# Layer 1 of a two-layer decoder: two low-rank inputs computed ahead of the norm, and the sample states of two heads read by one product

## The chip, the core and the metric

The kernel runs on one core of one Trainium2 chip. A core has TensorE (PE: matrix products, with its weight loads shown apart as PEld), VectorE (DVE), ScalarE (ACT), GpSimd (POOL) and SyncE (SP, which here issues most of the transfers). Engines run side by side and wait for one another on semaphores. TensorE writes to PSUM, which has 8 banks; the kernel numbers its PSUM results ("groups") through the program and gives group g the bank g mod 8. The metric is the device time of one execution in microseconds (us).

## What is computed

A two-layer trunk over 288 tokens of width 1024: 256 of one prompt and 32 of 8 samples with 4 tokens each. Layer 0 is a state-space and attention mixer with a dense feed-forward block; layer 1 is an RWKV-7 mixer with a mixture of 8 experts. The change lies in the layer 1 mixer, of which this is the part that matters:

```python
prev = jnp.concatenate([shift0[:, None].astype(h.dtype), h[:, :-1]], axis=1)   # h = rms(x) * norm_mix[1]
xx = prev - h
xr, xw, xk, xv, xa, xg = [h + xx * mu[i] for i in range(6)]
r = xr @ wr
k = xk @ wk
v = xv @ wv
w_log = -jax.nn.softplus(-(w0 + jnp.tanh(xw @ w1) @ w2).astype(f32)) - 0.5
a = jax.nn.sigmoid((a0 + (xa @ a1) @ a2).astype(f32))
g = jax.nn.sigmoid(xg @ g1) @ g2
...
def step(S, inp):                       # per sample and head, S is 64 x 64
    sa = jnp.einsum('bhvk,bhk->bhv', S, a_t)
    S = S * w_t[:, :, None, :] + sa[..., None] * b_t[:, :, None, :] + v_t[..., None] * k_t[:, :, None, :]
    return S, jnp.einsum('bhvk,bhk->bhv', S, r_t)
```

w1 and a1 are 1024 x 64, g1 is 1024 x 128; all is in 32-bit floats. Each mixed input is a share (1 - mu) of the token's own h and a share mu of the h of the token before it (of the stored shift state for the first token of a sample, of nothing for the first of the prompt).

## The kernel before

Activations lie feature-major: 8 tiles of 128 features by 288 tokens (KT = 8, T = 288, TP = 256 prompt tokens). Each engine runs a fixed list in its own order, so what stands first in the list goes first, and later entries wait behind it. PSUM groups are numbered by `stage` in one list (lines 515 to 530), and a group can be written when the group eight numbers before it has been freed. In the code `full(eng, g)` waits until TensorE has filled group g, `emptied(eng, g)` until a reader has freed it.

**The start of layer 1.** The last down projection of layer 0 (groups FD10, m = 0 to 7) is added to x tile by tile on DVE (`residual`, L1559). ACT squares each tile (L1017), DVE sums the squares (L1503), TensorE sums over the partitions in one product with ones (group N3), ACT makes the inverse root rs (L1028 Ln, L1031 Exp), and DVE writes h = x * norm * rs (L1493), the eight signals `h_tile`. DVE then copies the tokens that are shifted (L1849 to L1855). For the six mixed inputs n = 0 to 5 (w, a, g, k, r, v) ACT writes the own share into one of two buffers, `xi[n % 2]` (`own_share`, L1234), and DVE adds the share of the token before (`mix`, L1863 for the prompt, L1864 for the samples), signal `xi_ready`. TensorE takes them as they come: Hw (xw by w1), Ha (xa by a1), Rw (8 groups, the tanh of Hw by w2), Hg, Ra (8), Rg (8), then eight columns Rk0 to Rk7 of xk by wk, 16 records each, then r and v. ACT reads the hidden groups (L1240) and the outputs (L1247 with a sigmoid for w and a, L1249 for g). Its order is: own share 0, 1; hidden w; own share 2; hidden a; outputs w; own share 3; hidden g; outputs a; own share 4; outputs g.

Matrix products of 32-bit floats appear as two records each on PE and PEld, so 8 products give 16 records.

**The sample states.** Near the end of the mixer, the group sZY reads the 16 heads x 8 samples of states against the 4 tokens of a sample, for two vectors (2 x 4 = 8 columns). Two heads share 128 partitions, `r0` = 0 or 64:

```python
for i in range(KT):
    for s in range(DB):
        for r0 in (0, 64):
            ins = mm(zy[r0:r0 + 64, i * DB + s], wk[r0:r0 + 64, i, s, :],
                     AR[r0:r0 + 64, i, :, TP + DL * s:TP + DL * (s + 1)])
```

ACT copies the group out in two instructions (L1354, L1355). Ahead of it DVE masks the groups sA and sX (L1998, L2004), makes a constant and scales two inputs (`sE`, L2028, L2030) and adds a prompt state (L1984, L1991); behind it TensorE goes on with QZ(3,1), three transposes (L2650) and the rest of the chain. Then come the output projection and the experts, which fill the span from about 957 us on.

## Time and profile before

| | |
|---|---|
| median of 3 runs | 1747.38 us (1741.54 to 1748.83) |
| profiled execution | 1750.27 us, span of its core 1748.6 us |
| TensorE busy | 1683.8 us, 96% of the span |
| mean granted TensorE clock | 0.967 of full |
| chain of waits | PE 89%, DVE 7%, ACT 2% |

The page gives busy time by engine, the granted clock and the chain that ended last. Since one engine fills 96% of the span, what matters is where it waits, where its clock is halved, and what it is given to do. A timeline shows instructions in order of time, merged when alike: start, length from the first start to the last end, engine, line, operation, what is written from what, shape and count; in brackets the idle time before it and who ended it. For TensorE the shape 64\*128 means weights of 64 rows (partitions) by 128 columns.

### The profile page before, as it was taken

To read this page: it belongs to the slowest core of one execution; us is meant where nothing else is said; L and a number is where in the kernel's file an instruction comes from. 1 tells how busy PE (TensorE), PEld (TensorE's weight loads), DVE (VectorE), ACT (ScalarE), POOL (GpSimd) and SP (SyncE) were. 2 spreads that over 40 slices of the span, in tenths; PEclk is the share of its full clock that TensorE was granted. 3 is DMA by queue.
4 is the path that set the end of the run, shared out by engine and by line. 5 is a ranking of instruction groups with operands and counts; after the bars stand their busy time and mean duration, and the time that the engine had idled before them with its cause. 6 is when DMAs were issued, how large, how long until landed. Compare 5 with 4: busy or idle time off the path is not lost.

```text
span 1748.6 us, 25799 instructions
## 1 busy us (share of the span) xinstructions
PE 1683.8 (96%) x10101; PEld 1393.0 (80%) x10101; DVE 1177.0 (67%) x1525; ACT 918.6 (53%) x1193; POOL 148.0 (8%) x180
## 2 busy tenths in 40 slices
PE   9999699999997899999999999999999999999999
PEld 7776477999995677999867787888878787878787
DVE  5652722677657454444444788979797989888897
ACT  3442521543327243433223577767686868777774
POOL 1102100000000013322021200000000000000011
PEclk9999879999998999999797899999999999999999
DMA  8832422554322330000024989989797989899893
GB/s 349 356 133 86 199 97 103 224 194 155 145 86 97 123 118 0 2 1 2 2 103 169 393 335 380 411 326 423 313 427 312 423 355 383 356 380 392 348 421 142
DMA packets 41097, 405.03 MB, mean 232 GB/s; under 512 B 4784, under 2 KB 5072, under 8 KB 11664
## 3 DMA queue, kind: packets, MB, share of 16 engines
q1 hardware_dynamic: 34336, 372.64, 53.0%
q0 software_dynamic: 6672, 31.14, 4.4%
q8 instruction: 64, 1.05, 0.2%
q14 instruction: 25, 0.20, 0.0%
HBM read 379.49 MB, written 26.30 MB: 232 GB/s over the span
## 4 chain that ended last, share of the span: by engine, by line
PE 89%; DVE 7%; ACT 2%; issue 1%; DMA 1%; DVEq 0%; ACTq 0%; SPq 0%; POOL 0%; POOLq 0%
PE ps L2260 85%; DVE rest_ring L2072 1%; DMA ring<-in_moe_w 1%; PE ps L3010 1%; PE ps L2702 1%; PE ps L2650 1%; DVE ring L1553 0%; DVE arena L1522 0%; DVE arena L1648 0%; ACT arena L1151 0%; PE ps L2963 0%; DVE arena L1531 0%; PE ps L2928 0%; DVE arena L1661 0%; DVE arena L1527 0%
## 5 line engine op out<-in xcount | busy, mean ns | idle before, releaser
L2260 PE MATMUL ps<-head,hsel 128*128 128x512 f32 x1408 | 458.9, 397 | 4.5 <-DVE rest_ring L2072 4.5
L2072 DVE TENSOR_TENSOR rest_ring<-ring,head 128x2048 fp32r<-128x2048 f32 (+1 forms) x160 | 328.0, 2070 | 6.6 <-ACT head L1384 6.5
L2260 PEld LDWEIGHTS ps<-head,hsel 128*128 128x128 f32 x1408 | 265.0, 188 | 63.9 <-DVE rest_ring L2072 7.8
L2260 PE MATMUL ps<-arena,ring 128*128 128x288 f32 (+9 forms) x1552 | 276.8, 350 | 10.1 <-DVE arena L1864 6.6
L1384 ACT ACTIVATE head<-ring 128x2048 fp32r<-128x2048 f32 (+1 forms) x160 | 274.3, 1741 | 18.9 <-DMA ring<-in_moe_w 18.7
L2260 PEld LDWEIGHTS ps<-arena,ring 128*128 128x128 f32 (+4 forms) x1552 | 214.1, 200 | 69.8 <-issue 17.1
L2260 PE MATMUL ps<-rest_ring,hsel 128*128 128x512 f32 x576 | 225.0, 391 | 0.0
L2260 PE MATMUL ps<-head,actT_split 128*128 128x512 f32 x512 | 168.8, 393 | 7.4 <-issue 5.6
L2260 PE MATMUL ps<-rest_arena,head 128*128 128x288 f32 x704 | 174.7, 296 | 0.0
L2260 PE MATMUL ps<-rest_arena,rest_ring 128*128 128x288 f32 x528 | 155.5, 294 | 0.0
L2260 PE MATMUL ps<-h,ring 128*128 128x288 f32 (+2 forms) x624 | 135.2, 374 | 1.8 <-DVE h L1493 1.8
L2260 PEld LDWEIGHTS ps<-h,ring 128*128 128x128 f32 (+2 forms) x624 | 100.9, 179 | 35.7 <-issue 8.6
L2260 PEld LDWEIGHTS ps<-rest_ring,hsel 128*128 128x128 f32 x576 | 108.7, 189 | 20.8
L2260 PEld LDWEIGHTS ps<-rest_arena,head 128*128 128x128 f32 x704 | 122.5, 188 | 0.1
L2260 PEld LDWEIGHTS ps<-head,actT_split 128*128 128x128 f32 x512 | 96.1, 188 | 31.3 <-issue 8.4
L1559 DVE TENSOR_TENSOR x<-x,ps 128x288 f32<-128x288 f32 x110 | 48.7, 453 | 107.1 <-PE ps L2260 106.9
L2066 DVE TENSOR_TENSOR rest_ring<-ring,head 128x2048 fp32r<-128x2048 f32 x48 | 109.7, 2285 | 9.7 <-ACT head L1379 9.6
L2260 PE MATMUL ps<-arena 64*64 64x64 f32 (+12 forms) x1178 | 104.5, 295 | 10.7 <-DVE arena L1681 3.1
L2260 PE MATMUL ps<-rest_ring,actT_split 128*128 128x512 f32 x288 | 112.2, 390 | 0.0
L2260 PE MATMUL ps<-hsel,head 128*128 128x288 f32 x352 | 103.8, 295 | 0.0
L2260 PEld LDWEIGHTS ps<-arena 64*64 64x64 f32 (+6 forms) x1178 | 75.8, 164 | 30.3 <-issue 23.6
L2260 PEld LDWEIGHTS ps<-rest_arena,rest_ring 128*128 128x128 f32 x528 | 99.5, 188 | 0.0
(364 smaller groups left out, 2402.4 us busy)
## 6 DMA issues: line engine op xcount, KB each, us to landing
ring<-in_moe_w SPq DMA_DIRECT2D x72, 2048.0 KB, 11.1
ring<-in_moe_w SPq DMA_DIRECT2D x72, 1024.0 KB, 7.5
arena<-in_moe_w SPq DMA_DIRECT2D x16, 2048.0 KB, 14.3
ring<-in_ffn_w SPq DMA_DIRECT2D x11, 2048.0 KB, 7.4
arena<-in_moe_w SPq DMA_DIRECT2D x16, 1024.0 KB
ring<-in_ffn_w SPq DMA_DIRECT2D x11, 1024.0 KB, 5.0
moe_rows<-arena POOLq DMA_DIRECT2D x1, 6656.0 KB, 33.8
ring<-in_w_in SPq DMA_DIRECT2D x2, 3072.0 KB, 13.1
```

The lines of the kernel that those rows point to most:

```text
L1384: A(mhead[c % 2][:, o:o + w], mslot[s][:, o:o + w], ACT.Copy).then_inc(sem("gu_head"), 1)
L1559: V.tensor_tensor(x[:, m, :], x[:, m, :], bank(g)[:, 0:T], ALU.add).then_inc(freesem(g), 1)
L2066: V.tensor_tensor(mrest[s][:, GU:SLOT], mslot[s][:, GU:SLOT], down_head(c).bitcast(F32), ALU.subtract).then_inc(sem("dn_split"), 1)
L2072: V.tensor_tensor(mrest[s][:, o:o + w], mslot[s][:, o:o + w], mhead[c % 2][:, o:o + w].bitcast(F32), ALU.subtract).then_inc(sem("gu_split" ...
L2260: return nc.tensor.matmul(o, l, r, start=start, stop=stop, skip_group_check=skip)
L2650: ins = nc.tensor.transpose(b[0:rows, i * P:(i + 1) * P], src[:, 4 * hf + i, t0:t0 + rows], ident)
L2702: ins = nc.tensor.transpose(b[:, n * P:(n + 1) * P], (Mi if lv else Mti)[gg % 2][:, 4 * q + n, :], ident)
L3010: ins = nc.tensor.transpose(turned(c)[:, u * P:(u + 1) * P], actm[c % 2][:, u * P:(u + 1) * P], ident)
```

## The change

**Hidden products ahead of the norm.** rs is one number per token, so it can be multiplied in after the product. For w and a, ACT writes raw = x * norm into `xi[0]` beside each square. DVE makes from w1 and from a1 one 128-column weight each: 64 columns scaled by 1 - mu, 64 by mu (four instructions, placed in the last pass but one over the feed-forward chunks). One product of 288 columns per tile gives both shares of all tokens, one of 8 columns the shift state's share. DVE (`joined_hidden`) scales both halves by rs and adds the second, shifted by one token, to the first. Own shares and mixes of w and a are gone. The tanh moves to its own instruction on ACT; Ra stands before Hg.

**sZY.** DVE clears and fills `ar_both`, in which each head's 8 columns stand beside 8 columns of zeros, so one product with weights of 128 rows by 64 columns gives both heads of a pair of partitions (16 columns). ACT copies out in eight instructions.

```diff
@@ scalar
-            squares(sq3, x, lambda k: emptied(act, base[f"FD{FC - 1}"] + k), "sq_ready")
+            for k in range(KT):
+                emptied(act, base[f"FD{FC - 1}"] + k)
+                A(sq3[:, k, :], x[:, k, :], ACT.Square).then_inc(sem("sq_ready"), 1)
+                A(raw[:, k, :], x[:, k, :], ACT.Copy, scale=v("nm1", k)).then_inc(sem("h_head"), 1)
...
-            own_share(0)
-            own_share(1)
-            hidden("w", ACT.Tanh)
+            emptied(act, base["Hw"])
+            A(hid[0][0:64, :], hid[0][0:64, :], ACT.Tanh).then_inc(sem("hid_tanh"), 1)
             own_share(2)
-            hidden("a", ACT.Copy)
             lora_out("w", sw, "w0")
+            lora_out("a", aT, "a0")
             own_share(3)
             emptied(act, base["Rw"] + 7)
             hidden("g", ACT.Sigmoid)
-            lora_out("a", aT, "a0")
             own_share(4)
             lora_out("g", gT, None)
...
+                    zy = bank(g).rearrange("p (i b r a l) -> p i b r a l", b=DB, r=2, a=2, l=DL)
+                    for i_, dst in enumerate((z1T, y1)):
+                        for u in range(2):
+                            for r in range(2):
+                                ins = A(dst[64 * r:64 * r + 64, u:KT:2, :].rearrange("p k (b l) -> p k b l", l=DL),
+                                        zy[64 * u:64 * u + 64, :, :, r, i_, :], ACT.Copy)
@@ vector
+                if c == FC - 1:
+                    loaded(dve, "lora")
+                    o = VEC["mu"][0]
+                    for nm, mrow, at in (("w", 1, 0), ("a", 4, 512)):
+                        for i, share in enumerate((ommu[:, 8 * mrow:8 * mrow + 8], vec[:, o + 8 * mrow:o + 8 * mrow + 8])):
+                            V.tensor_tensor(both_shares(nm)[:, :, i, :], W("lora")[:, at:at + 512].rearrange("p (k n) -> p k n", k=KT),
+                                            share.unsqueeze(2).broadcast_to([P, KT, 64]), ALU.mult).then_inc(sem("shares_ready"), 1)
...
+            def joined_hidden(nm, dst):
+
+                g = base["H" + nm]
+                full(dve, g)
+                b = bank(g)
+                old = prev_hid[:, TP:T].rearrange("p (b l) -> p b l", l=DL)
+                V.tensor_tensor(prev_hid[:, 1:TP], b[64:P, 0:TP - 1], rs[0][64:P, 0:TP - 1], ALU.mult)
+                V.tensor_tensor(old[:, :, 1:DL], b[64:P, TP:T].rearrange("p (b l) -> p b l", l=DL)[:, :, 0:DL - 1],
+                                rs[0][64:P, TP:T].rearrange("p (b l) -> p b l", l=DL)[:, :, 0:DL - 1], ALU.mult)
+                V.tensor_copy(old[:, :, 0], b[64:P, T:T + DB])
+                link(V.tensor_tensor(dst[0:64, :], b[0:64, 0:T], rs[0][0:64, :], ALU.mult))
+                V.tensor_tensor(dst[0:64, 1:T], dst[0:64, 1:T], prev_hid[:, 1:T], ALU.add).then_inc(freesem(g), 1)
+                emptied(dve, g)
...
+            joined_hidden("w", hid[0])
+            for k in range(KT):
+                V.scalar_tensor_tensor(h[:, k, :], x[:, k, :], v("nm1", k), rs[0], ALU.mult, ALU.mult).then_inc(sem("h_tile"), 1)
+            joined_hidden("a", hid[1])
...
-            for n in range(5):
-                mix(n)
+            mix(2)
+            V.tensor_copy(shiftout[:, :, 0], h[:, :, TP - 1]).then_inc(sem("shiftout_ready"), 1)
+            V.tensor_copy(shiftout[:, :, 1:9], hs[:, :, :, 3]).then_inc(sem("shiftout_ready"), 1)
+            mix(3)
+            mix(4)
...
+                    for r in range(2):
+                        V.memset(ar_both[64 * r:64 * r + 64, :, 1 - r], 0.0)
+                        V.tensor_copy(ar_both[64 * r:64 * r + 64, :, r], AR[64 * r:64 * r + 64, :, :, TP:T]).then_inc(sem("ends_scaled"), 1)
@@ tensor
+            pe.wait_ge(sem("shares_ready"), 4)
+            pe.wait_ge(sem("x_half_loaded"), 32)
+            both_hidden("w")
+            summed(base["N3"], 2, sq3, C("ones"))
+            both_hidden("a")
             lora_out(0, "w")
+            lora_out(1, "a")
+            loaded(pe, "lora")
             hidden(2, "g")
-            lora_out(1, "a")
             lora_out(2, "g")
...
+                    pe.wait_ge(sem("ends_scaled"), 2)
+                    zy = b.rearrange("p (n r a l) -> p n r a l", r=2, a=2, l=DL)
                     for i in range(KT):
                         for s in range(DB):
-                            for r0 in (0, 64):
-                                ins = mm(zy[r0:r0 + 64, i * DB + s], wk[r0:r0 + 64, i, s, :],
-                                         AR[r0:r0 + 64, i, :, TP + DL * s:TP + DL * (s + 1)])
+                            r0 = 64 * (i % 2)
+                            ins = mm(zy[r0:r0 + 64, i // 2 * DB + s], wk[:, i, s, :], ar_both[:, i, :, :, DL * s:DL * (s + 1)])
```

The order of TensorE around the norm of layer 1, before; the last rows of the feed-forward block, N3 (one product with the constants `cst`), then Hw and Ha (64x288) and Rw, Hg, Ra, Rg and the first columns' products (128x288):

```order
L2260 MATMUL ps<-rest_arena,head 128x288 x2
L2260 MATMUL ps<-rest_arena,rest_ring 128x288
L2260 MATMUL ps<-arena,cst 128x288
L2260 MATMUL ps<-arena,ring 64x288 x16
L2260 MATMUL ps<-arena,ring 128x288 x48
```

And of the change, the same place; the pair of rows with `shiftst` stands eight times ahead of N3 and eight times behind it:

```order
L2306 MATMUL ps<-rest_arena,head 128x288 x2
L2306 MATMUL ps<-rest_arena,rest_ring 128x288
L2306 MATMUL ps<-arena,ring 128x288
L2306 MATMUL ps<-shiftst,ring 128x8
...
L2306 MATMUL ps<-arena,cst 128x288
L2306 MATMUL ps<-arena 128x288
L2306 MATMUL ps<-shiftst,arena 128x8
...
L2306 MATMUL ps<-arena,ring 128x288 x48
```

Hw now stands ahead of N3 and Ha behind it, both with 128 weight columns, and neither waits for h any longer.

The order of ACT from the inverse root (`rs`) to the outputs of g, before:

```order
L1031 ACTIVATE rs<-rs 128x288
L1035 ACT_TABLE_LOAD
L1234 ACTIVATE arena<-h,arena 128x288 x16
L1240 ACTIVATE arena<-ps 64x288
L1234 ACTIVATE arena<-h,arena 128x288 x8
L1240 ACTIVATE arena<-ps 64x288
L1247 ACTIVATE arena<-ps,vec 128x288 x8
L1234 ACTIVATE arena<-h,arena 128x288 x8
L1240 ACTIVATE arena<-ps 128x288
L1247 ACTIVATE arena<-ps,vec 128x288 x8
L1234 ACTIVATE arena<-h,arena 128x288 x8
L1249 ACTIVATE arena<-ps 128x288 x8
```

And of the change:

```order
L1041 ACTIVATE rs<-rs 128x288
L1045 ACT_TABLE_LOAD
L1264 ACTIVATE arena<-arena 64x288
L1246 ACTIVATE arena<-h,arena 128x288 x8
L1259 ACTIVATE arena<-ps,vec 128x288 x16
L1246 ACTIVATE arena<-h,arena 128x288 x8
L1252 ACTIVATE arena<-ps 128x288
L1246 ACTIVATE arena<-h,arena 128x288 x8
L1261 ACTIVATE arena<-ps 128x288 x8
```

Sixteen own-share rows are gone, and the hidden row of g (L1252) now stands behind both sets of sigmoids and an own share.

## Rows read from the trace of the kernel before

**Rows 1.** The page: busy time, share of the span and instructions by engine.
```profile
PE 1683.8 (96%) x10101; PEld 1393.0 (80%) x10101; DVE 1177.0 (67%) x1525; ACT 918.6 (53%) x1193; POOL 148.0 (8%) x180
```
**Rows 2.** Stretches: length, then busy PE, PEld, DVE, ACT, POOL, clock, DMA.
```profile
533.60:539.70 6.10, 0.00 (x0) 0.00 (x0) 5.37 (x22) 6.04 (x13) 0.55 (x1) 0.50 0.69 293
539.70:543.80 4.10, 4.03 (x9) 2.07 (x10) 4.10 (x15) 2.69 (x7) 0.00 (x0) 0.50 0.01 2
543.80:549.50 5.70, 5.70 (x25) 3.08 (x23) 5.70 (x22) 3.63 (x9) 0.00 (x0) 1.00 0.00 0
```
**Rows 3.** Timeline of PE around the norm: start, length, instruction, idle before.
```profile
530.13 0.29 PE L2260 MATMUL ps<-rest_arena,rest_ring 128*128 128x288 f32 x1
532.40 0.75 PE L2260 MATMUL ps<-arena,cst 128*128 128x288 f32 x2 [1.98 <-DVE arena L1503]
539.77 26.25 PE L2260 MATMUL ps<-arena,ring 128*64 128x288 f32 x96 [6.62 <-DVE arena L1864]
566.26 4.12 PE L2260 MATMUL ps<-arena,ring 128*128 128x288 f32 x16 [0.25 <-issue]
```
**Rows 4.** Timeline of DVE, last splits, residuals, norm, and copies.
```profile
518.39 0.88 DVE L1835 TENSOR_TENSOR rest_arena<-arena,rest_arena 128x288 fp32r<-128x288 f32 x2
519.19 0.81 DVE L1559 TENSOR_TENSOR x<-x,ps 128x288 f32<-128x288 f32 x2
...
524.18 0.45 DVE L1559 TENSOR_TENSOR x<-x,ps 128x288 f32<-128x288 f32 x1 [0.34 <-PE ps L2260]
...
534.26 3.52 DVE L1493 SCALAR_TENSOR_TENSOR h<-x,vec,rs 128x288 f32<-128x288 f32 x8 [1.92 <-ACT rs L1031]
```
**Rows 5.** Timeline of ACT, own shares, outputs with sigmoid, hidden g.
```profile
550.42 3.90 ACT L1247 ACTIVATE arena<-ps,vec 128x288 f32<-128x288 f32 x8 [0.28 <-PE ps L2260]
554.22 3.50 ACT L1234 ACTIVATE arena<-h,arena 128x288 f32<-128x288 f32 x8
557.96 0.41 ACT L1240 ACTIVATE arena<-ps 128x288 f32<-128x288 f32 x1 [0.23 <-PE ps L2260]
```
**Rows 6.** Timeline of PEld, the loads of Rw and Hg.
```profile
549.64 3.69 PEld L2260 LDWEIGHTS ps<-arena,ring 64*128 64x128 f32 x16 [0.44 <-issue]
553.71 3.69 PEld L2260 LDWEIGHTS ps<-arena,ring 128*128 128x128 f32 x16 [0.39 <-issue]
```
**Rows 7.** Timeline of PEld, weight loads with few columns to multiply: four places.
```profile
842.78 0.58 PEld L2260 LDWEIGHTS ps<-arena 64*32 64x32 f32 x32
...
846.30 12.69 PEld L2260 LDWEIGHTS ps<-arena,ring 64*64 64x64 f32 x255
...
875.95 1.08 PEld L2260 LDWEIGHTS ps<-ring 32*32 32x32 f32 x32
...
929.32 3.20 PEld L2260 LDWEIGHTS ps<-router,h 128*128 128x128 f32 x28 [0.81 <-issue]
```
**Rows 8.** Stretches around sZY, columns as in Rows 2.
```profile
846.30:847.60 1.30, 1.30 (x53) 1.30 (x51) 0.98 (x3) 0.00 (x0) 0.00 (x0) 1.00 0.00 0
847.60:859.00 11.40, 11.40 (x217) 11.38 (x214) 3.86 (x7) 0.00 (x0) 0.00 (x0) 0.50 0.01 3
859.00:868.00 9.00, 9.00 (x47) 6.30 (x47) 4.93 (x9) 4.78 (x9) 0.00 (x0) 0.50 0.00 0
```
**Rows 9.** Timeline of DVE and ACT around sZY.
```profile
844.40 0.29 DVE L2028 SCALAR_TENSOR_TENSOR arena<-cst 128x128 f32<-128x128 f32 x1
...
846.57 0.85 DVE L1984 TENSOR_TENSOR h<-ring,ps 64x256 f32<-64x256 f32 x2 [1.21 <-PE ps L2260]
...
848.34 0.68 DVE L2036 TENSOR_TENSOR ring<-arena,cst 32x512 f32<-32x512 f32 x1
...
859.13 0.38 ACT L1354 ACTIVATE arena<-ps 128x256 f32<-128x256 f32 x1 [13.11 <-PE ps L2260]
...
862.91 0.59 ACT L1298 ACTIVATE h<-ps 64x512 f32<-64x512 f32 x1 [3.12 <-PE ps L2260]
```

More of the change, by code:

```diff
@@ L277, in decoder_trunk @@
         hid = tm1
+        raw = xi[0]
+        prev_hid = Us[0:64, 0:T]
         xxf = xx[:, :, :].rearrange("p k t -> p (k t)")
@@ L287, in decoder_trunk @@
         centre = xxf[:, 2048:2048 + P]
+        ar_both = AR[:, :, 1, 0:P].rearrange("p k (r a t) -> p k r a t", r=2, a=2)
         def gn_unit(n):
@@ L366, in decoder_trunk, with both_shares @@
         slots = ar[:, 3 * SLOT + 3 * P:3 * SLOT + 4 * P]
+        def both_shares(nm):
+            o = (where["lora"] % RING) * SLOT + 5120
+            t = ring[:, o:o + 1024] if nm == "w" else xi2[:, KT * T:KT * T + 1024]
+            return t.rearrange("p (k s n) -> p k s n", k=KT, s=2)
         def down_head(c):
@@ L517, in decoder_trunk @@
         stage("N3", 1)
-        for name, n in (("Hw", 1), ("Ha", 1), ("Rw", 8), ("Hg", 1), ("Ra", 8), ("Rg", 8)):
+        for name, n in (("Hw", 1), ("Ha", 1), ("Rw", 8), ("Ra", 8), ("Hg", 1), ("Rg", 8)):
             stage(name, n)
@@ L1352, in _ @@
                     full(act, g)
-                    zy = bank(g).rearrange("p (n a l) -> p n a l", a=2, l=DL)
-                    A(z1T.rearrange("p k (b l) -> p (k b) l", l=DL), zy[:, :, 0, :], ACT.Copy)
-                    A(y1.rearrange("p k (b l) -> p (k b) l", l=DL), zy[:, :, 1, :], ACT.Copy).then_inc(freesem(g), 1)
+                    zy = bank(g).rearrange("p (i b r a l) -> p i b r a l", b=DB, r=2, a=2, l=DL)
[4 more added lines that the diff above has]
+                                        zy[64 * u:64 * u + 64, :, :, r, i_, :], ACT.Copy)
+                    ins.then_inc(freesem(g), 1)
                 elif name == "sVT":
@@ L1844, in _ @@
             sum_squares(sq3, 24, KT - 1)
-            norm(base["N3"], "nm1", "h_tile")
+            def joined_hidden(nm, dst):
[10 more added lines that the diff above has]
+                emptied(dve, g)
+            emptied(dve, base["N3"])
+            n_norm[0] += 1
+            dve.wait_ge(sem("rs_ready"), n_norm[0])
+            joined_hidden("w", hid[0])
+            for k in range(KT):
+                V.scalar_tensor_tensor(h[:, k, :], x[:, k, :], v("nm1", k), rs[0], ALU.mult, ALU.mult).then_inc(sem("h_tile"), 1)
+            joined_hidden("a", hid[1])
             dve.wait_ge(sem("h_tile"), 2 * KT)
             dve.wait_ge(sem("x_half_loaded"), 32)
-            V.tensor_copy(shiftout[:, :, 0], h[:, :, TP - 1]).then_inc(sem("shiftout_ready"), 1)
             hs = h[:, :, TP:T].rearrange("p k (b l) -> p k b l", l=DL)
-            V.tensor_copy(shiftout[:, :, 1:9], hs[:, :, :, 3]).then_inc(sem("shiftout_ready"), 1)
             hp = hprev.rearrange("p k (b l) -> p k b l", l=DL)
@@ L1891, in _ @@
             mix(5)
-            dve.wait_ge(sem("xi_ready"), 48)
+            dve.wait_ge(sem("xi_ready"), 32)
             for t in range(KT):
@@ L2598, in _ @@
                         done(ins, g)
-            summed(base["N3"], 2, sq3, C("ones"))
-            loaded(pe, "lora")
             lw = W("lora")
@@ L2604, in _, with both_hidden @@
             l2 = {"w": 2048, "a": 3072, "g": 4096}
+            shift_now = shiftst
+            def both_hidden(nm):
+                g = base["H" + nm]
+                w = both_shares(nm).rearrange("p k s n -> p k (s n)")
+                b = take(g)
+                for k in range(KT):
+                    if nm == "w":
+                        pe.wait_ge(sem("h_head"), KT + k + 1)
+                    mm(b[:, 0:T], w[:, k, :], raw[:, k, :], k == 0, k == KT - 1, skip=True)
+                    ins = mm(b[:, T:T + DB], w[:, k, :], shift_now[:, k, :], False, k == KT - 1, skip=True)
+                done(ins, g)
             def hidden(n, nm):
@@ L2607, in hidden @@
                 w = lw[:, o:o + KT * rows].rearrange("p (k n) -> p k n", k=KT)
-                proj(base["H" + nm], w, 0, rows, xi[n % 2], rows=rows, ready="xi_ready", n0=8 * n)
+                proj(base["H" + nm], w, 0, rows, xi[n % 2], rows=rows, ready="xi_ready", n0=8 * (n - 2))
             def lora_out(n, nm):
@@ L2612, in lora_out @@
                 emptied(pe, base["H" + nm])
+                if nm == "w":
+                    pe.wait_ge(sem("hid_tanh"), 1)
                 for m in range(KT):
@@ L2616, in lora_out @@
                     done(mm(b[:, 0:T], lw[0:rows, l2[nm] + m * P:l2[nm] + (m + 1) * P], hid[n % 2][0:rows, :]), g)
-            hidden(0, "w")
-            hidden(1, "a")
+            pe.wait_ge(sem("shares_ready"), 4)
[3 more added lines that the diff above has]
+            both_hidden("a")
             lora_out(0, "w")
+            lora_out(1, "a")
+            loaded(pe, "lora")
             hidden(2, "g")
-            lora_out(1, "a")
             lora_out(2, "g")
@@ L2633, in column @@
                 w = W(f"w{nm}{t // 4}").rearrange("p (k n) -> p k n", k=KT)
-                proj(g, w, t % 4 * P, P, xi[n % 2], ready=None if t else "xi_ready", n0=8 * n)
+                proj(g, w, t % 4 * P, P, xi[n % 2], ready=None if t else "xi_ready", n0=8 * (n - 2))
             for t in range(KT):
```

15 lines of the change are left out of this document (7 added, 8 removed).

## The prediction

> **What bounds the kernel.** I read the page first: TensorE is busy in 96% of the span [rows 1]. A change can pay only where that engine waits, where it runs at half clock, or where it gets less to do. The timeline of PE shows one such place at the start of layer 1: between the last product of layer 0 (530.13 + 0.29 = 530.42) and the first column Rk0 (566.26) lie 35.84 us, in which it waits 1.98 us for the sum of squares and 6.62 us for norm, own share and mix [rows 3]. The stretches say more: the clock falls to 0.50 (1.2 instead of 2.4 GHz) in the gap and is still there in the first 4.1 us of Hw and Ha [rows 2]. From 543.8 on TensorE is full. The second place is sZY: 255 records fill 12.69 us [rows 7], nearly all at clock 0.50, and 9.0 us behind it are at 0.50 too [rows 8]. From 566 to 840 nothing is touched, so what is won at Rk0 is passed on as a shift.
>
> **Part one, step by step.** The steps are dated from 530.42, at full clock.
> Hw: each tile is two records of 288 columns and two of 8. The first cost 4.12 / 16 = 0.26 [rows 3], rather 0.25 with the pipeline's tail off. The second are nowhere beside long ones; the nearest row has 128 weight columns against 8 columns and takes 3.20 / 28 = 0.114 each [rows 7]. Bounds are 0 (the load hides behind the long product) and 0.114; I take the upper, since behind a short product the next load has no cover. 8 x (0.50 + 0.23) = 5.8 us, to 536.2. This is work where there was a gap. Its raw tiles come in time: square and scaled copy take less than the 0.8 us that the next residual needs.
> N3 now stands behind Hw and starts at 536.2 instead of 532.40: the norm is put off by 3.8 us. From the start of N3 to the start of the norm it was 534.26 - 532.40 = 1.86 us [rows 3, 4], so rs is there at 538.1. DVE joins w in five instructions, two of them full rows and one of 255 columns (near 0.45, as a residual [rows 4]), two tiny: 1.6 us, bounds 1.2 and 2.5; then tanh, 0.4. All of this is under Ha, which runs from 536.7 to 542.5.
> From there ACT sets the pace. Its list is own share 2 (it overwrites the raw tiles, so it waits for Ha), 16 sigmoids, own share 3, hidden g: 3.5 + 2 x 3.8 + 3.5 + 0.4 = 15.0 us (3.8 is the step from 550.42 to 554.22) [rows 5], from 542.6 to 557.6. TensorE meanwhile does Rw, then Ra as ACT frees banks (to 550.5), then Hg, 4.1 us (553.71 - 549.64 [rows 6]), to 554.6. There it waits **3.0 us** for hidden g: what is late next, in place of the wait for the mix. Rg takes 4.1 more, and Rk0 starts at 561.9 instead of 566.26: **-4.4 us**, bounds -2.9 and -6.6 by the two ends of the short records and the join.
> DVE is not late: join a to 544.8, copies 1 us, mix 2 (4.5 us as now) to 550.3, before Ra is done.
> The 3.0 us wait may cost clock. Before, a gap was followed by 4.1 us of work at 0.50 [rows 2], which costs at most half of that, 2.0 us. This gap is shorter and stands between full stretches; I take **+1.0**, bounds 0 and 2.0.
> The four scaling instructions on DVE have 512 columns, 0.68 each [rows 9], 2.7 us, put ahead of the first residual at 519.19. Their cover is the bank of that group, which is wanted again only when the eighth group is done, some 0.8 us behind each other; the eighth residual starts at 524.18 [rows 4], so the first bank is wanted at about 523.8, and it will be free at 522.4. Cost 0; if they took twice as long, 1 to 2 us of feed-forward would wait. The removed own shares and mixes (16 x 0.43 on ACT, 2 x 4.5 on DVE) are counted above by their absence.
>
> **Part two, sZY.** The products halve from 128 to 64, records from 256 to 128. Whether the time does is the main question. Before, neighbours alternate between rows and columns 0 to 63 and 64 to 127; afterwards eight in a row use all rows and the same 64 columns. The rows on weight loads: 32 columns, alternating between two row halves, 0.58 / 32 = 0.018 per record; 32 columns always at the same place, 1.08 / 32 = 0.034; 128 columns at the same place, 0.114 [rows 7]. So records at different places run two at a time, and a record alone takes about as long as its columns are many. For 64 columns that is between 0.034 and 0.114, about 0.06 at full clock; and at half clock the pair took 2 x 0.050 = 0.10 [rows 7, 8]. A record of the change thus costs what a **pair** cost, and there are as many as there were pairs. Time at the same clock: unchanged, 7.7 us at full and 13 at half against 12.69. I take **0**, bounds -2 and +1 by how much of it falls at full clock.
> The Trainium skill, page TensorEngine Tiling (Array Packing), section Tiling Modes (Key Properties), says that different tiles of the array can load weights and multiply in parallel; this speaks against the change, for it trades two small tiles for one larger. The pairs of rows 7 agree with it. By a count of instructions alone the sum would be 6.4 us lower.
> Filling `ar_both` puts four instructions of 512 columns ahead of sZY on DVE, from 844.40 on [rows 9]: two clears and two copies, 0.45 to 0.68 each, together 1.8 to 2.7 us, so they end between 846.2 and 847.1, against a start of sZY at 846.30. **+0.3**, bounds 0 and 0.8. Behind them wait the constant, the two scalings and the state's addition L1984 (846.57), which QZ(3,1) needs only after sZY: 10 us of cover. The ACT copies become eight, near 0.25 each (0.38 is for 256 columns [rows 9]): 2.0 instead of 0.7, done at about 861.2, ahead of the next one at 862.91. Cost 0; with a sZY at full clock 1 us would show.
>
> **Sum.** -4.4 + 1.0 + 0 + 0.3 = -3.1 us. Against the profiled execution that is 1750.27 - 3.1 = 1747.2; against the median, which is 2.9 lower, 1747.38 - 3.1 = **1744.3 us**. Half-clock stretches elsewhere may fall otherwise by 1 or 2 us either way.
>
> **Rivals.**
> A, the count decides: 128 records at 0.050 take 6.4 us, so another -6.3: 1738.0. For it: 12.69 / 255 is what a record took. Against: the single-place rows. 0.14.
> B, the clock stays at full in sZY, since a record now multiplies 16 columns on 128 rows. Then sZY takes 7.7 us instead of 12.7, and the 9.0 us behind shrink by up to 4.5, of which ACT's eight copies and its queue of evictions eat 1: -8.5, 1735.8. Against: long weight loads and little to multiply in both versions. 0.09.
> C, the slower end: the clock falls during Rw and Ra. They now stand together, 8 us with weights of 64 rows, where Hg with 128 rows stood between them. At 0.50 each takes 8.2 instead of 4.1 us: Rw to 550.7, Ra to 558.9, with ACT behind it; own share 3 and hidden g to 563.0, Rg at least 4.1: Rk0 at 567.3 or later, +1.0, with the clock's return +1.0 and +0.3 for sZY: 1749.7. It decides if the stretch 542 to 550 shows 0.50 for more than 5 us. For it: such a change of order. Against: Ha with 64 weight columns brought the clock back to 1.00 at 543.8 [rows 2]. 0.08.
> D, nothing is gained since the norm chain is just later: TensorE would need to wait again after Ha. That takes rs more than 3 us later than 538.1; time 1747.5. 0.05.
>
> **How the numbers follow.** My forecast has 0.58, between 1740 and 1747.5; 0.06 is for what I have not seen. The range 1735.5 to 1749.5 takes in A, B and most of C. A measurement of this kernel can tell about 0.5%, or 8.7 us, from no change. Faster by more than that (below 1738.6) are most of A, B and a tail of my own case: 0.23. Slower by more needs C and a second mishap: 0.04. The rest, 0.73, is within.
>
> **What will show it.** In the profile after: Hw starts right behind the last feed-forward product, about 5.8 us long; N3 near 536; no wait behind Ha; one wait near 3 us ahead of Rg, ended by ACT; Rk0 near 562. sZY with 128 records in 11 to 13.7 us, at 0.50 mostly; its start within 1 us after the last product ahead of it. I am wrong if the records of sZY come at 0.050 and below at clock 0.50, if its clock is 1.00, or if TensorE waits somewhere else between Hw and Rk0.

## The result

| kernel | median us | lowest to highest | profiled execution us | its mean granted clock |
|---|---|---|---|---|
| before | 1748.1 | 1740.8 to 1751.2 (8 runs) | 1750.27 | 0.967 |
| after | 1732.55 | 1729.6 to 1737.0 (8 runs) | 1732.14 | 0.979 |

The ratio is 0.9916, interval 0.990 to 0.993: 15.6 us faster, where I had forecast 3.1, and 3 us below the lower end of my range. The page of the changed kernel begins:

```profile
span 1730.5 us, 25591 instructions
## 1 busy us (share of the span) xinstructions
PE 1668.6 (96%) x10005; PEld 1383.3 (80%) x10005; DVE 1175.0 (68%) x1511; ACT 914.4 (53%) x1190; POOL 143.5 (8%) x180
```

Its PE is busy for 15.2 us less than in [rows 1], and waits for 3 us less. The timeline of PE in the changed kernel, from the last product of layer 0 on (columns as in rows 3):

```profile
526.88 0.29 PE L2306 MATMUL ps<-rest_arena,rest_ring 128*128 128x288 f32 x1
527.01 0.65 PE L2306 MATMUL ps<-arena,ring 128*128 128x288 f32 x2
527.49 0.28 PE L2306 MATMUL ps<-shiftst,ring 128*128 128x8 f32 x2
...
532.59 0.73 PE L2306 MATMUL ps<-arena,cst 128*128 128x288 f32 x2
...
538.82 12.35 PE L2306 MATMUL ps<-arena,ring 64*128 64x288 f32 x48
552.41 11.91 PE L2306 MATMUL ps<-arena,ring 128*128 128x288 f32 x48 [1.25 <-ACT arena L1252]
565.15 0.75 PE L2306 MATMUL ps<-arena,cst 128*128 128x288 f32 x2 [0.83 <-ACT arena L1281]
```

Hw begins at once, N3 stands behind it, Ha, Rw, Ra and Hg follow without a gap, and one wait of 1.25 us for hidden g is left ahead of Rg. The waits of 1.98 and 6.62 us of [rows 3] are gone. But the first row shows something else as well: the last product of layer 0, which the change does not touch, is 3.25 us earlier than in [rows 3] (530.13). ACT in the same place:

```profile
538.92 3.52 ACT L1246 ACTIVATE arena<-h,arena 128x288 f32<-128x288 f32 x8 [2.46 <-PE ps L2306]
542.34 6.34 ACT L1259 ACTIVATE arena<-ps,vec 128x288 f32<-128x288 f32 x16
548.48 3.58 ACT L1246 ACTIVATE arena<-h,arena 128x288 f32<-128x288 f32 x8
551.88 0.47 ACT L1252 ACTIVATE arena<-ps 128x288 f32<-128x288 f32 x1
```

These are own share 2, the 16 sigmoids, own share 3 and hidden g, back to back: what is late next is ACT, as forecast, only by less. The stretches (us, busy PE, PEld, DVE, ACT, POOL, clock, DMA share, GB/s), over the whole place and in sZY, and the loads of sZY:

```profile
527.00:575.00 48.00, 45.08 (x200) 34.51 (x198) 32.62 (x103) 27.02 (x64) 0.55 (x1) 1.00 0.26 98
...
838.00:840.50 2.50, 2.50 (x54) 2.50 (x55) 2.42 (x7) 0.00 (x0) 0.00 (x0) 1.00 0.02 7
840.70:846.60 5.90, 5.90 (x73) 5.90 (x73) 2.98 (x5) 0.00 (x0) 0.00 (x0) 0.50 0.00 1
```

```profile
837.96 8.85 PEld L2306 LDWEIGHTS ps<-arena,ring 128*64 128x64 f32 x128
846.68 1.61 PEld L2306 LDWEIGHTS ps<-ring,arena 128*64 128x64 f32 x8
```

The clock is 1.00 through the whole of part one, where [rows 2] has 10 us at 0.50. sZY takes 8.85 us instead of the 12.69 of [rows 7].

**Where the 18.1 us between the two profiles lie.** The same product is looked for in both timelines, and its start in the one is subtracted from its start in the other. The last two columns are two further profiles, of the kernel before once more (e7_before) and of the kernel with part one alone (e1_part_one), both told of below, against the same profile of before.

| product | after | e7_before | e1_part_one |
|---|---|---|---|
| last of layer 0 | -3.3 | -3.5 | -0.9 |
| behind Rk1 (575.09 in before) | -9.9 | -3.2 | -7.6 |
| last products ahead of sZY (845.9) | -8.5 | -3.0 | -7.5 |
| behind sZY (859.01) | -12.3 | -3.2 | -7.6 |
| ahead of the last norm (946) | -13.2 | -3.5 | -7.9 |
| behind the 48 products after it (971) | -23.4 | -12.1 | -16.4 |
| first group of the experts (1001) | -19.3 | -9.7 | -13.9 |
| end | -18.1 | -9.7 | -13.2 |

The column of e7_before is the key. The same instructions as in my profile of before come out 9.8 us shorter in another execution: 3.5 in layer 0 and 6.2 between 946 and 1001. The change has 6.7 us in part one and 3.7 in sZY with the wait ahead of it; it loses 1.4 between the two, where the half-clock stretch near 660 is 6.8 us long instead of 3.4 (at 670 in before). The other 9.1 us are about what a kernel that was not changed shows too. So a difference of two profiles does not give what the change is worth, and each part was run by itself.

### The profile page after: what moved, and what is told of

It reads as the page before. It is cut to its first block, busy times and chain, and to the rows that moved or that the text cites. A ratio compares the mean times of both kernels' runs of the same rounds, so it can differ in the third digit from the quotient of the medians.

```text
span 1730.5 us, 25591 instructions
## 1 busy us (share of the span) xinstructions
PE 1668.6 (96%) x10005; PEld 1383.3 (80%) x10005; DVE 1175.0 (68%) x1511; ACT 914.4 (53%) x1190; POOL 143.5 (8%) x180
## 4 chain that ended last, share of the span: by engine, by line
PE 87%; DVE 5%; DMA 3%; ACT 2%; issue 2%; POOL 0%; SPq 0%; DVEq 0%; ACTq 0%; POOLq 0%
PE ps L2306 83%; DMA ring<-in_moe_w 2%; DVE rest_ring L2118 1%; PE ps L2766 1%; PE ps L3074 1%; DMA out_s_wkv<-ring 1%; PE ps L2714 1%; DVE ring L1567 0%; DVE arena L1536 0%; DVE arena L1662 0%; ACT arena L1161 0%; ACT arena L1246 0%; ACT arena L1259 0%; PE ps L3027 0%; DVE arena L1545 0%
## 5 line engine op out<-in xcount | busy, mean ns | idle before, releaser
L2306 PE MATMUL ps<-arena,ring 128*128 128x288 f32 (+9 forms) x1408 | 267.6, 357 | 4.5 <-DVE arena L2061 1.7
L2306 PEld LDWEIGHTS ps<-arena,ring 128*128 128x128 f32 (+4 forms) x1408 | 207.0, 196 | 58.7 <-issue 7.1
L2306 PE MATMUL ps<-arena 64*64 64x64 f32 (+11 forms) x1194 | 102.0, 287 | 11.0 <-DVE arena L1695 3.1
## 6 DMA issues: line engine op xcount, KB each, us to landing
arena<-in_moe_w SPq DMA_DIRECT2D x16, 1024.0 KB, 13.2
```

Of the source, the lines that this page charges most:

```text
L2306: return nc.tensor.matmul(o, l, r, start=start, stop=stop, skip_group_check=skip)
```

## Experiments

"Before" is 1748.6 us (median of 29 runs), 1748.4 in the later comparisons.

**The two parts alone.** e1_part_one is the changed kernel with sZY, its copies out and its DVE filling as they were:

```diff
-                            r0 = 64 * (i % 2)
-                            ins = mm(zy[r0:r0 + 64, i // 2 * DB + s], wk[:, i, s, :], ar_both[:, i, :, :, DL * s:DL * (s + 1)])
+                            for r0 in (0, 64):
+                                ins = mm(zy[r0:r0 + 64, i * DB + s], wk[r0:r0 + 64, i, s, :],
+                                         AR[r0:r0 + 64, i, :, TP + DL * s:TP + DL * (s + 1)])
```

> The changed kernel with sZY as it was: the 256 small products, no ar_both, two copies out. Part one of the change alone. Theory A (part one is worth more than I forecast, because its terms were too large, and the rest of the gain is sZY and the places of the half-clock stretches): in the two traces the distance from the last feed-forward product of layer 0 to Rk0 shrank by about 6.6 us (35.8 to 29.2) with the clock at 1.00 throughout; so the time is that of the kernel before less 6.6, about 1741.5 us, ratio 0.996, and the span between Rk0 and sZY is unchanged but for half-clock stretches. Theory B (the half-clock stretches at 270.7 us and from 946.6 us, which the changed kernel does not show, are gone because of part one): less 6.6, less another 6 to 8, about 1734 us, ratio 0.992, and the trace shows 1.00 at 270 and from 930 to 960. Theory C (my forecast of part one was right and the clock behind the gap costs 1 us): 1745, ratio 0.998, with a stretch at 0.50 between 545 and 565.

Measured: 1741.65 us (1735.3 to 1747.4), ratio 0.998, interval 0.996 to 1.000. From the last product of layer 0 to the one behind Rk1 the shift is -7.6 + 0.9 = -6.7 us, as in the changed kernel. Theory A holds. The clock stands at 1.00 there, so C is out, and the stretch at 270 us is there again, so B is out.

e2_samples is the same edit the other way round, on the kernel before.

> The kernel before with the change to sZY alone: 128 products of 128 rows instead of 256 of 64, ar_both filled by DVE, eight copies out. Theory A (a record of the change is cheaper than a pair was: 0.047 instead of 0.051 us at clock 1.00 and 0.082 instead of 0.105 at 0.50): sZY takes between 6.0 us at full clock and 10.5 us at half instead of 12.7, so the time is lower by 2 to 4.5 us, about 1744.5, ratio 0.998. Theory B (a record costs what a pair did, the step as I forecast it, and the 3.8 us that sZY lost in the changed kernel came from the clock falling 1.3 us later in it): sZY between 11 and 13.7 us here if the clock falls at its start, time within 1 us of the kernel before. Theory C (the half-clock stretches from 930 us on depend on sZY): a further 5 us, about 1739, and clock 1.00 from 930 to 960.

Measured: 1738.97 us (1735.5 to 1743.4), ratio 0.995, interval 0.994 to 0.997. Its sZY takes 9.84 us, and the clock falls 1.4 us after its start, as it did before: so the record itself is cheaper (A). But the median is lower by 9.7 us, and a profile that shows 2.7 us won from the work ahead of sZY to the work behind it does not pay for that. Neither A nor B gave this; the 5 us of C are there in the median, and the clock is at 1.00 from 934 to 974, but the cause is not yet shown. The loads of sZY:

```profile
847.09 9.84 PEld L2269 LDWEIGHTS ps<-arena,ring 128*64 128x64 f32 x128
```

**A record's neighbour.** e3_halves changes the order of the changed kernel's 64 products in sZY, and nothing else:

```diff
-                    for i in range(KT):
-                        for s in range(DB):
+                    for i0 in range(0, KT, 2):
+                        for s, i in ((s, i) for s in range(DB) for i in (i0, i0 + 1)):
```

> The changed kernel with sZY's 128 products in another order: neighbours now alternate between the two column halves (heads i and i+1 for each sample) where eight in a row used the same half. Nothing else differs. Theory A (records at the same rows but different columns also load side by side, and the pace of 0.047 us at full and 0.082 at half clock is that of a record alone): the records come at about 0.03 at full and 0.055 at half clock, sZY takes 4 to 7 us instead of 8.85, time 2 to 4 us under the changed kernel, about 1729.5. Theory B (only records in different row halves run side by side, and now all rows are in each): sZY as in the changed kernel, 1732.5 us, ratio to before 0.991.

Measured: 1726.1 us (1723.0 to 1728.4), ratio 0.989: 6.4 us under the changed kernel. Its loads of sZY and the stretch in it:

```profile
837.30 3.84 PEld L2306 LDWEIGHTS ps<-arena,ring 128*64 128x64 f32 x128
```

```profile
837.40:841.00 3.60, 3.60 (x126) 3.60 (x127) 3.50 (x9) 0.00 (x0) 0.00 (x0) 1.00 0.02 7
```

A record takes 3.60 / 127 = 0.028 us, against 2.50 / 55 = 0.045 in the changed kernel, both at full clock. And the clock doesn't fall, neither in sZY nor in the 28 us behind it (the next 0.50 is at 869), so besides the 5.0 us of sZY itself another 3.4 us are won behind it against the changed kernel (4.3 against before). Theory A, and more than it said. (In the texts of e1_part_one, e2_samples and e3_halves and in the next I called "products" what the rows count as records: an fp32 product is two of them, so sZY is 128 products and 256 records before, 64 and 128 after.) The Trainium skill, page TensorE: Matmul & The Clock Gate, section The mechanism, says that a weight load overlaps only when its row group differs from that of the product under way; here every record has all 128 rows, and 0.028 against 0.045 us says that another column half is enough, so on this point the measurement decides against the page. The Trainium skill, page TensorEngine Tiling (Array Packing), section Key Properties, says that different tiles load and multiply in parallel; the run agrees. (The other column half also writes the other half of the PSUM partitions; no run separates the two.)

e5_one_place takes the alternation away from the kernel before (`for r0 in (0, 64)` outside `for s in range(DB)`).

> The kernel before with the 256 products of sZY in another order: eight samples in a row on rows and columns 0 to 63, then eight on rows and columns 64 to 127, where neighbours alternated. Same products, same results. Theory A (neighbours at different places of the array run side by side; a record at the same place as the one before costs 0.047 us at clock 1.00 and 0.08 at 0.50, whether it has 64 or 128 rows): sZY takes nearly twice as long, 256 x 0.08 = 20 us at half clock instead of 12.6, and the time is 7 or 8 us above the kernel before in the same case of its clock, 1749 to 1758. Theory B (a record costs 0.05 us wherever its neighbour stands, and the gain of the last experiment, 8.9 to 3.8 us, came from something else): sZY 12 to 13 us as before.

Measured: 1748.89 us in one run; the loads of sZY and its stretches:

```profile
844.47 19.07 PEld L2260 LDWEIGHTS ps<-arena,ring 64*64 64x64 f32 x256
```

```profile
844.60:847.30 2.70, 2.70 (x63) 2.70 (x60) 2.46 (x6) 0.00 (x0) 0.00 (x0) 1.00 0.00 0
847.50:863.40 15.90, 15.90 (x197) 15.90 (x196) 2.18 (x4) 0.00 (x0) 0.00 (x0) 0.50 0.01 2
```

With 64 rows at the same place a record takes 2.70 / 60 = 0.045 and 15.90 / 196 = 0.081 us, the same as the changed kernel's records of 128 rows (0.045; 5.90 / 73 = 0.081). Theory A: the rows don't count, the neighbour does. A pair of alternating records of [rows 8] took 2 x 1.30 / 51 = 0.051 and 2 x 11.38 / 214 = 0.106. So at full clock the changed record is 12% cheaper than the pair that it replaces, at half clock 24%. With 6.5 us more in sZY it is 8.4 us above e7_before, but only at the median of before: again a time that the work alone doesn't give.

**The order around Hg.** e6_hg_early is e3_halves with Hg ahead of Ra on TensorE (its PSUM number too, which is not shown), and own share 3 and hidden g ahead of the sigmoids of a on ACT:

```diff
             lora_out(0, "w")
-            lora_out(1, "a")
             loaded(pe, "lora")
             hidden(2, "g")
+            lora_out(1, "a")
...
             lora_out("w", sw, "w0")
-            lora_out("a", aT, "a0")
             own_share(3)
             emptied(act, base["Rw"] + 7)
             hidden("g", ACT.Sigmoid)
+            lora_out("a", aT, "a0")
```

> The kernel e3_halves with the gate's first product Hg ahead of Ra (as in the kernel before) and, on ACT, own share 3 and hidden g between the sigmoids of w and of a. Theory A (what is late ahead of Rg is only ACT's queue: hidden g stands behind 16 sigmoids and own share 3): Hg follows the mix of its input tile by tile and ends near 547.8, hidden g ends under Ra, TensorE does not wait for it, and Rk0 starts 1.2 us sooner; 1725 us against 1726.1, the gap of 1.24 us ahead of Rg is gone, the clock stays at 1.00 from 530 to 560. Theory B (moving ACT's work makes the banks late: Rg finds its banks not emptied, or Hg waits for the mix for more than it gives back): a wait of 1 us or more in another place between Ha and Rk0, time 1726 or above. Theory C (weights of 64 rows in Rw and Ra, with Hg between them, or without, decide on the clock): a stretch at 0.50 in one of the two orders; the changed kernel and e3_halves showed none, so C is the less likely. This run also repeats e3_halves in effect: its time must again lie 5 to 8 us under the changed kernel (1732.55).

Measured: 1725.07 us (1722.8 to 1727.9), not to be told from 1726.1 by its times. The rows tell: TensorE from the end of Rg on, PEld in the same place (Rg, then Rk0), and ACT.

```profile
554.64 0.65 PE L2306 MATMUL ps<-arena,ring 128*128 128x288 f32 x2
555.85 8.00 PE L2306 MATMUL ps<-arena,ring 128*128 128x288 f32 x32 [0.56 <-issue]
```

```profile
551.14 3.69 PEld L2306 LDWEIGHTS ps<-arena,ring 128*128 128x128 f32 x16 [0.39 <-issue]
555.82 1.27 PEld L2306 LDWEIGHTS ps<-arena,ring 128*128 128x128 f32 x6 [0.99 <-issue]
```

```profile
551.89 3.56 ACT L1246 ACTIVATE arena<-h,arena 128x288 f32<-128x288 f32 x8
555.29 2.55 ACT L1261 ACTIVATE arena<-ps 128x288 f32<-128x288 f32 x8
```

The wait ahead of Rg is gone, and in its place TensorE waits ahead of Rk0 (0.56 us), whose bank, by the times, the first gate copy empties at about 555.6; that copy stands behind own share 4 in ACT's queue. Hg itself now follows DVE's mix tile by tile and takes 4.4 instead of 4.1 us. Part one has 38.07 us here against 38.27 in e3_halves (from the last product of layer 0 to the one behind Rk1): of 1.2 us, 0.2 came through. Theory B, in a milder form. By the times, ACT's queue ends the last wait of this place in either order.

**Where the other 6 us come from.** e4_before, e7_before and e8_before are the kernel before, unchanged.

> The kernel before once more, for a second profile of the same instructions. Theory A (where the clock stands at 0.50 outside the wait ahead of Rk0 and outside sZY differs from one execution to the next of the same program): the stretches at 270.7 us (6.8 us long), 670.1, 892 to 903 and 946.6 (27.3 us) are found elsewhere, shorter, or not at all, while those at 533 and 848 are found again. Theory B (they belong to the program): all of them are found again at the same place within 1 us and as long. The time is 1748 us in either case.

> The kernel before, one more profile. Its 29 times of the last comparison lie in two groups, 12 from 1740.6 to 1742.5 at a mean clock of 0.975 and 16 from 1747.5 to 1751.6 at 0.969 to 0.965. Theory A (the groups differ by where TensorE's clock is at 0.50 from 930 to 975 us: the 48 products of 128 x 128 take 8.5 us there at 1.00 and 15.0 at 0.50): an execution of 1741 shows no stretch at 0.50 longer than 3.4 us behind 930, one of 1749 to 1751 shows one of 20 us or more there. Theory B (they differ in sZY or in layer 0): the long stretch behind 930 is there in neither or both, and the difference of 8 us stands at another place.

> As e7_before: the kernel before once more, so that both groups of its times may be seen. Theory A: the profile's time follows from the length of the half-clock stretch behind 930 us. Theory B: it follows from another place.

Measured: 1748.6 us as median of e4_before (its profile 1745.7), 1740.49 and 1741.59 for the other two. In e4_before three of the stretches that I had named are within 1.5 us of where the profile of before has them (272.2, 671.6, 948.1); that of 892.0 begins at 890.1 and is 6.8 us long instead of 3.4, and the last is 3.4 us long instead of 27.3:

```profile
948.10:951.50 3.40, 3.40 (x19) 3.40 (x18) 2.02 (x15) 1.84 (x4) 0.56 (x1) 0.50 0.36 75
```

Neither theory as it was put, and enough to show that its length is no property of the program. Of 71 times of the kernel before in all comparisons, 23 lie between 1740.6 and 1743.2 (clock 0.975 or 0.976 where it is on record), 43 between 1747.1 and 1752.0 (0.969 to 0.965), and 5 between. Stretches of the profile of before ahead of and in the 27.3 us in question, then those of e7_before:

```profile
943.20:946.60 3.40, 3.40 (x22) 2.07 (x20) 1.80 (x4) 1.21 (x3) 0.00 (x0) 1.00 0.00 0
946.60:973.90 27.30, 26.07 (x95) 21.41 (x94) 9.88 (x30) 9.25 (x14) 0.56 (x1) 0.50 0.84 324
```

```profile
943.70:947.10 3.40, 3.40 (x19) 3.40 (x18) 2.06 (x15) 1.84 (x4) 0.56 (x1) 0.50 0.37 75
947.10:974.40 27.30, 23.30 (x123) 18.51 (x123) 19.24 (x45) 14.84 (x16) 3.80 (x2) 1.00 0.95 375
```

In both the clock falls at the sums of squares of the last norm. In the one it stays down for 27.3 us and the 48 products behind the norm are done at half clock, in the other it is back after 3.4 us. Those 48 products in the profile of before, then in e7_before, then in the changed kernel:

```profile
956.13 15.03 PE L2260 MATMUL ps<-arena 128*128 128x128 f32 x48 [0.97 <-ACT arena L1415]
```

```profile
950.62 8.48 PE L2260 MATMUL ps<-arena 128*128 128x128 f32 x48 [1.23 <-ACT arena L1415]
```

```profile
939.30 8.48 PE L2306 MATMUL ps<-arena 128*128 128x128 f32 x48 [1.23 <-ACT arena L1429]
```

Theory A of e7_before holds for the place behind 946: 8.5 us are lost there, of which 2.3 are given back where TensorE waits for the experts' weights afterwards. But B is right too: another 3.5 us of the difference lie in layer 0, where stretches at 0.50 lie elsewhere from the start on (the one at 270.7 in before begins at 267.9 in e7_before). So part of what separates the groups is there ahead of the change's place, and more of it is paid behind. This rests on one profile of the upper group (before) against two of the lower (e7_before, e8_before: last product of layer 0 at 526.6 and 526.8); e4_before, whose 1745.7 lies in neither, leaves layer 0 latest of all (531.1) and yet has the short stretch.

No profile of a kernel whose sZY differs (after, e2, e3, e5, e6) shows the stretch at the last norm at all; all five with the old sZY (before, e1, e4, e7, e8) do, at 3.4 or 27.3 us. Is it the new form of sZY, or only that the program arrives at another instant? e9_sixteen and e10_thirtytwo add work to the kernel before, e12_after_pad to the changed one:

```diff
-                    for i in range(KT):
+                    for i in [0] + list(range(KT)):
```

(`[0, 1]` in the other two.) Here the same slip of counting: they repeat 32, 64 and 32 records, 1.6, 3.4 and 2.6 us at half clock, twice what the texts say.

> The kernel before with 16 of sZY's 256 products done twice (the 16 of the first head pair, ahead of the rest, same results): 0.8 us more work at half clock, 0.4 at full, and nothing else. In its profiles so far the clock falls in all five with the old sZY at neighbours alternating (for 27.3 us in one, 3.4 in four) near the sums of squares of the last norm, and in none with sZY changed or reordered. Theory A (whether it falls there, and for how long, hangs on at what instant the program arrives, so that a shift of under 2 us decides): the times no longer lie in two groups at 1741 and 1749 in the shares 13 to 25; the share of executions above 1747 changes, and the profile shows the stretch at 946 gone or longer. Theory B (the changed sZY takes it away because of what it is, or because it is shorter): the two groups stay with their shares, both 0.8 us later; median 1749.4.

> As e9_sixteen, with 32 products done twice: 1.6 us more work at half clock. Theory A (the instant decides): with more work the kernel can be faster than the kernel before: if the stretch near 946 us is gone, 1742 to 1744, at a mean clock of 0.974 or more. Theory B: both groups of times 1.6 us later, median 1750.2.

> The changed kernel with 16 of sZY's 128 products done twice: 1.3 us more at half clock. Theory A (the instant of arrival decides on the stretch near the last norm, which the changed kernel's executions, 1729.6 to 1737, never show): the shift may bring it: 1733.8 from the work alone, and executions at 1737 to 1742, with a stretch at 0.50 at about 935. Theory B (it is sZY's new form that takes the stretch away): 1733.8, none of them above 1738.

Measured for e9_sixteen: 1746.48 us, twelve times from 1743.9 to 1748.4 in one group, ratio 0.999 (0.998 to 1.001). sZY is 1.6 us longer (14.30), and the stretch is gone:

```profile
845.11 14.30 PEld L2260 LDWEIGHTS ps<-arena,ring 64*64 64x64 f32 x287
```

```profile
947.00:974.00 27.00, 23.88 (x133) 19.18 (x132) 17.82 (x56) 12.48 (x16) 2.62 (x3) 1.00 0.82 318
```

More work, the same products, and neither the group at 1741 nor any time above 1748.5. So the stretch can go without a new form of sZY, by a shift alone, as theory A has it (whether the repeated records act by the delay or by what they make TensorE do, no run separates). It is not the whole of the difference: the lower group plus 1.6 us would be 1743.1, and 1746.5 was measured.

Measured for e10_thirtytwo: 1754.03 us (1747.2 to 1756.2), and with 3.4 us more in sZY both groups are back, 3 times at 1747 to 1748.7 and 9 at 1753 to 1756.2; its profile has the long stretch again:

```profile
950.30:977.60 27.30, 26.34 (x94) 21.56 (x94) 10.12 (x27) 9.99 (x14) 0.57 (x1) 0.50 0.82 316
```

For this kernel I had expected the opposite of the long stretch under A, since I had the size of the shift wrong; what it shows is that another shift brings the stretch back.

e12_after_pad: 1738.27 us (1735.1 to 1740.9), sZY 9.92 us, no stretch near the last norm. Theory B allowed no time above 1738, and three of six are; theory A allowed them but asked for the stretch: one shift of the changed kernel was not enough to bring it, so that its new sZY keeps the stretch away is not ruled out. It adds 5.7 us to the median for 1.1 in sZY; most of the rest stands at other half-clock stretches (in layer 0 its profile is 3.4 us behind that of the changed kernel, which no edit explains).

Nor does the instant alone sort the profiles. The sums of squares of the last norm start at 946.5 in e9_sixteen (no stretch), 946.9 in before (27.3 us), 947.8 in e4_before (3.4), 950.1 in e10_thirtytwo (27.3) and 950.7 in e5_one_place (none). A shift can move a program from one case to the other; by what rule, stays open.

**Do the parts add?** e11_samples_halves has the order of e3_halves without part one.

> The kernel before with sZY as in e3_halves (128 products of 128 rows, neighbours at different column halves), without part one. Theory A (the two parts add, and a record at another place than its neighbour costs 0.030 us): sZY takes 3.8 to 5 us and the clock stays at 1.00 in it and behind it; from the faster group of before (1741.2) less 8.7 for sZY and 4 for the 9 us behind it that were at half clock: 1728.5; and with part one it would be the 1726.1 and 1725.1 of e3_halves and e6_hg_early less nothing, so the parts would not add, or it is 1726.1 + 6.2 = 1732.3 if they do. I expect 1732. Theory B (the clock falls anyway, since the products behind sZY are as small): 1736 or more, with a stretch at 0.50 of 10 us or more between 845 and 870.

Measured: 1731.92 us (1729.6 to 1733.3), against the 1732 I expected; sZY 3.84 us, no fall of the clock till 875. With part one 1726.1: 5.8 us for part one, against 6.4 between e2_samples and the changed kernel and 6.7 in the traces. They add.

## Why the prediction was wrong

Three steps failed, two of them sizes: in part one, 3.3 us too small, ACT's price above all (1.6 of it) and the clock's return (1.0); in sZY, 4.0 us too small, the price of a record alone at half clock; and the base, with its allowance of 1 or 2 us for the clock elsewhere. With the two sizes right the sum would have been 1747.4 - 6.7 - 3.7 = 1737.0, still in the range; the third put the time outside it.

**The base, and "half-clock stretches elsewhere may fall otherwise by 1 or 2 us either way"**: the three times I had (1741.54, 1747.38, 1748.83) already lay in the two groups, and I took their middle one as the kernel's own time. From the median of before, 1748.1, the work of the two parts and the 1.4 us given back near 660 make 1739.1, 6.6 us above the measured 1732.55, where the allowance was 1 or 2. From the lower group, 1741.5, the same sum makes 1732.5. That this meets the measurement within 0.1 us is partly luck: it leaves out the 0.9 us that the table shows between sZY and the last norm. The lower group and the measured work also give e2_samples (1738.8, measured 1739.0), but they make 1721.8 for e3_halves (1726.1) and 1728.6 for e11_samples_halves (1731.9), both with the 4.3 us won behind sZY, 1743.1 for e9_sixteen (1746.5) and 1732.1 for e12_after_pad (1738.3), 3 to 6 us too little. What is shown is that executions of the same instructions lie up to 10 us apart by where the clock is halved, and that added work alone makes the groups go (e9_sixteen) and come back (e10_thirtytwo). Why the changed kernel's eight times show no upper group is not shown. A range that took in one group more on either side, 8 us, would have held the result.

**Part one**: the mechanism was right at each step, the size was not: -6.7 where the sum had -4.4 + 1.0. Hw was 5.6 us long for my 5.8 (0.71 for each tile but the first), so the short records cost nearly the upper bound; join (1.6 us) and tanh (0.4) as forecast; Ha was done 0.5 us sooner. The four scaling instructions took 2.5 us ahead of the first residual and cost nothing, as forecast: TensorE does not wait in the rows ahead of Hw. The step that failed is ACT's price. I took 3.8 us for eight sigmoids from the step of [rows 5]. There ACT followed TensorE's products of Rw one by one, 4.1 us for eight; freed of that, 16 took 6.34 us, 3.2 for eight. Own shares and the rest were 0.3 us shorter. 15.0 us became 13.4, the wait for hidden g 1.25 instead of 3.0 us, and Rk0 came 2.3 us sooner than I had it. That ACT paces this place is borne out by e6_hg_early, where most of the wait only moved.

**The clock behind the wait**, +1.0: nothing. The stretch from 527 to 575 is at 1.00, and so it is in e1, e3 and e6. In [rows 2] TensorE had been idle for 6.6 us at a stretch, now for 1.25; that this is the reason was not tested.

**sZY**, "a record of the change thus costs what a pair cost ... I take 0, bounds -2 and +1": -4.0 us, from 12.76 to 8.76 between its first product and the next group's. The step from rows alternating to rows alone was right at full clock within 12% (0.045 for 0.051; I had said 0.06). At half clock, where most of it runs, I had no row of a record alone and took the pair's price; a record alone is 0.081 there. For the 77 or so records at half clock that is 77 x 0.025 = 1.9 us, and 0.3 more for those at full clock. Of the remaining 1.8 about 1.4 are the clock, which falls 2.6 instead of 1.3 us after the start (1.3 us at full clock do the work of 2.7 at half); 0.4 stays unassigned. In e2_samples it falls after 1.4 us, and 3.0 us are left, of which the records' price is 2.7 (100 x 0.025 and 27 x 0.006), so the two causes stand apart.

**Filling ar_both**, +0.3: right. The last rows ahead of sZY before, then after, with DVE's last copy:

```profile
845.83 0.54 PEld L2260 LDWEIGHTS ps<-arena 64*64 64x64 f32 x15
846.24 0.13 PEld L2260 LDWEIGHTS ps<-arena,ring 64*64 64x64 f32 x1
```

```profile
837.29 0.55 PEld L2306 LDWEIGHTS ps<-arena 64*64 64x64 f32 x16
837.42 0.42 DVE L2073 COPY arena<-arena 64x512 f32<-64x512 f32 x1
```

DVE is done at 837.84, and sZY starts 0.12 us later, at 837.96; so it does in the other profiles with ar_both (e2, e3, e11, e12). From the group ahead to sZY it is 0.67 us instead of 0.41. With this the 4.0 us are the 3.7 of the table.

**The eight copies** took 2.25 us for my 2.0, and ACT was idle for 1.43 us behind them: hidden, as forecast. In e3_halves, where sZY is at full clock, ACT has no idle time behind them any more.

**The rivals.** A (the count decides, 0.050 a record) named the right place and sign, but for the wrong reason: per record the cost did not stay, it rose from 0.0255 to 0.045 at full clock. B: the clock held for 1.3 us more, not throughout; it held throughout in e3_halves, and there it was worth what I had priced it at, 4.3 us behind sZY. C and D did not come: no 0.50 between 527 and 575, no wait behind Ha.

## What to carry to other kernels

When a kernel's few given times lie apart by more than the measurement of one of them, look for groups before taking the middle: put each time beside its mean clock, and widen the range by their distance: here 1.6 us of added work made the groups go and 3.4 us brought them back. Small fp32 products that follow each other should stand at different places of TensorE's array, where another column half is enough; the changed kernel gained 6.4 us more when its loop alternated between the column halves. An engine's step read where it follows another engine is the other engine's step, so look for a row where nothing holds it up.

## What the runs showed of the hardware

- Loads of 64 fp32 columns with few columns to multiply: 0.045 us a record at the same place at full clock and 0.081 at half, for 64 rows and 128 alike; with neighbours at another row half (and column half) 0.0255 and 0.053, at another column half with all rows 0.028 at full.
- With the records at 0.028 us the clock did not fall in sZY or in the 28 us behind it (e3, e6, e11); with the same products at 0.045 it fell 1.4 to 4.6 us after the start (e2, after, e12), and with those of before after 1.3 to 1.6.
- The same instructions took 1740.5 to 1750.3 us in four profiles; between the two ends 3.5 us came from half-clock stretches in layer 0 and 6.2 from one at the last norm, 3.4 or 27.3 us long. What decides between them in an execution stays open.
- The last product of layer 0 starts between 526.6 and 531.1 us in all fourteen profiles, whatever was changed behind it.
